# Who subtracts the low parts of the weights: GpSimd or VectorE, in a two-layer hybrid decoder step

## The chip, the cores and the metric

The kernel is one program on one core of a Trainium2 chip. The metric is the device time of one execution in microseconds (us); three runs of the kernel before gave 2476.75, 2478.96 and 2480.17, and their median, 2478.96, is the time before.

## What is computed

Two layers, each of them: a half-step SwiGLU feed-forward, a token mixing step, another half-step SwiGLU. The mixing step multiplies the normed input by one wide matrix and cuts the product into parts: z, the 4096 convolution channels (x, B, C), dt, the attention's q, k, v and two gates. The convolution channels feed a state-space scan (SSD); q, k, v feed a dilated window attention; both results are gated, added and multiplied by a last matrix.

```python
z, xbc, dt_raw, q, k, v, g_ssd, g_attn = split_cols(u @ w_in, IN_SIZES)
conv = silu(conv_b + sum(xbc_full[:, i:i + seqlen] * conv_w[i] for i in range(4)))
y, new_ssm = ssd_scan(xs5, dt, a_head, bmat, cmat, ssm_state)     # 8 groups of 4 heads
y = grouped_rmsnorm((y + d_skip * xs5) * silu(z), ssd_norm, 8)
merged = sigmoid(g_ssd) * (y @ w_ssd_out) + sigmoid(g_attn) * (attn @ w_attn_out)
return merged @ w_o, ...
```

All is float32. There are 256 prompt tokens and 32 tokens of the second group, 288 columns in all.

## The kernel before

The weights pass through the core once. They come in *units* of 128 x 2048 numbers (1 MB), two at a time in the two slots s = 0 and 1 of `raw`, `w_hi` and `w_lo`. A unit's way is always the same, and each step has a semaphore of its own per slot:

- SP loads it into `raw[s]` once the low part of the slot's last unit is made (`unit`, L494 to L498, waits for `lo_ready[s]`).
- ScalarE rounds it into `w_hi[s]` once TensorE is done with the slot's last unit (`high_unit`, L669 to L672; signal `hi_ready[s]`).
- An engine subtracts, `w_lo = raw - w_hi` (`low_unit`; signal `lo_ready[s]`). VectorE has one at L920 to L924, GpSimd has another at L1334 to L1337.
- TensorE multiplies (`product`, L1412 to L1417): three matmuls for each block, `w_hi` by the input's high part, `w_hi` by its low part, `w_lo` by its high part. At the end it signals `unit_done[s]`.

While TensorE works on one slot, the other slot's next unit is prepared. Every engine runs its own list in order; nothing is reordered, and a wait holds all that stands behind it on the engine. The order is written out by hand.

A layer passes through these stages: the first feed-forward; q, k, v and dt; the convolution channels (16 units, `xbc`, between steps of the attention); eight state-space groups (each with three half units of z and gate columns, `side`); a tail (gate units, the sums for the grouped norm, the attention's output matrix, four pairs of `w_ssd_out`, two of `w_o`); the second feed-forward.

In the feed-forwards and the q, k, v stage VectorE makes all low parts. In the other stages GpSimd makes many:

- Convolution: VectorE's `xbc(n)` (L1088) makes the unit of slot 0 at its head when n is even; GpSimd loops over the eight units of slot 1 (L1377). `xbc(n)` then copies the convolution's tails (L1092) and applies four taps to two channel tiles (L1103 the first, L1106 the rest); its last tap lets ScalarE apply silu (L738). At the stage's end ScalarE's copies to `conv_out` (L827) stand behind the last silu.
- Groups: all units by GpSimd (`side_low`, L1386), one after each group and one more in odd groups, between its output DMAs (L1396 of the prompt's state, L1400 of the sample states).
- Tail: all units by GpSimd, in a loop of nine pairs (L1402).

VectorE's part of one group (from L1200) is, in order: `a_tri` (L1207 to L1214) for TensorE's product L1779; `xdt`, `cbm`, `xdte` (L1222 to L1235); for the group before, rows times silu of z (`times_z`, L1194 to L1198); `b_diag` (L1242); the decay matrices times `cbm` (L1248, L1250, signal `m_ready`), for which TensorE's product L1799 waits; then the outputs (L1255 to L1264), the new states (L1271) and the sample rows (L1276 to L1282), which let the next group start. ScalarE makes the exponentials for L1248 from the result of L1779 to L1784; meanwhile TensorE has the matmul L1790 and a half unit.

In the tail VectorE makes `y` ready in four parts: reciprocal (L1294), four scalings (L1297), split into high and low (L933, L935). After the second part it waits for the attention's output product and multiplies it with its gate (L1305). After the last pair of `w_ssd_out` come the merging (L1312, L1317, split), the residual sum (`add_to_x`, L985), the next norm (L954, L958, L950).

Of the kernel before, what the change touches and what calls it, by code (L numbers as in the profile page):

```python
# [40 lines left out]
G = 8  # L41
# [33 lines left out]
PAIRS_SO, PAIRS_AO, PAIRS_WO = 4, 1, 2  # L75
# [3 lines left out]
M_XBC = M_QKV + PAIRS_QKV  # L79
# [104 lines left out]
def trunk(nc, x_prompt, x_sample, cache_kv_w128, cache_kv_w512, cache_kv_w2048, state_conv, state_ssm,  # L184
# [163 lines left out]
    with ExitStack() as ctx:  # L348
# [570 lines left out]
        def _(dve):  # L919
# [87 lines left out]
            with dve.Fori(0, DEPTH) as l:  # L1007
# [78 lines left out]


                def xbc(n):  # L1088
                    if n % 2 == 0:
                        low_unit(0, m + (M_XBC + n // 2 + 1))  # L1090
                    wait(dve, xbc_taken, l, 2 * n + 2)
                    dve.tensor_copy(tails[:, 2 * n:2 * n + 2], flat[:, 2 * n:2 * n + 2, TP:TP + 9 * RUN]  # L1092
                                    .rearrange("p t (j c) -> p t j c", c=RUN)[:, :, :, 0:CW - 1])\
                        .then_inc(tails_ready.sem, 1)
                    if n:
                        wait(dve, xbc_ready, l, n)
                    for w in range(CW):
                        for t in range(2):
                            tile = 2 * n + t
                            src, dst = flat[:, tile, w:w + CONVED], acc[:, t, 0:CONVED]  # L1100
                            tap = conv_wt[:, w * KC + tile:w * KC + tile + 1]
                            if w == 0:
                                dve.tensor_scalar(dst, src, tap, vecs[:, V_CONVB + tile:V_CONVB + tile + 1],  # L1103
                                                  ALU.mult, ALU.add)
                            else:
                                last = dve.scalar_tensor_tensor(out=dst, in0=src, scalar=tap, in1=dst,  # L1106
                                                                op0=ALU.mult, op1=ALU.add)
                        if w < CW - 1:
                            dve.drain()
                    last.then_inc(conv_ready.sem, 1)  # L1110
# [83 lines left out]
                def times_z(g):  # L1194

                    wait(dve, silu_z_ready, l, g + 1)
                    rows_y = flat[:, 2 * g:2 * g + 2, 0:T]
                    dve.tensor_tensor(rows_y, rows_y, silu_z[:], ALU.mult).then_inc(z_used.sem, 1)  # L1198

                for g in range(G):  # L1200
                    heads = slice(HPG * g, HPG * g + HPG)

# [35 lines left out]
                        .then_inc(xdt_ready.sem, 1)  # L1238
                    if g:
                        times_z(g - 1)  # L1240
                    wait(dve, b_ready, l, g + 1)
                    dve.tensor_tensor(b_diag[:], b_tm_s[:].unsqueeze(1).broadcast_to((TS, NB, NS)),  # L1242
                                      sel_s.unsqueeze(2).broadcast_to((TS, NB, NS)), ALU.mult)\
# [3 lines left out]
                    for c in range(2):  # L1247
# [2 lines left out]
                    dve.tensor_tensor(dec_s[:], dec_s[:], cbm_s[:].unsqueeze(1).broadcast_to((TS, HPG, TS)), ALU.mult)\  # L1250
                        .then_inc(m_ready.sem, 1)

                    wait(dve, y_product, l, g + 1)
                    off = ps[:, 1, 0:256].rearrange("p (t c) -> p t c", t=2)
                    dve.tensor_tensor(off_t[:], off, e_off[:], ALU.mult)  # L1255
# [29 lines left out]
                    last.then_inc(y_read.sem, 1)  # L1285
                dve.drain().then_inc(rows_used.sem, 1)
                times_z(G - 1)

                wait(dve, y_rms_ready, l, 1)
                wait(dve, conv_done_out, l, 32)  # L1290
                wait(dve, h_end_out, l, 16 * G)
                for n in range(PAIRS_SO):
# [8 lines left out]
                    if n == 1:  # L1301

                        wait(dve, unit_done[1], l, M_AO + 1)
                        for o in range(0, KD, 2):
                            dve.tensor_tensor(gates[:, KD + o:KD + o + 2, :], ps[:, o:o + 2, 0:T],  # L1305
                                              gates[:, KD + o:KD + o + 2, :], ALU.mult).then_inc(row_evac.sem, 1)


                wait(dve, gates_ready, l, 1)
                wait(dve, unit_done[1], l, M_SO + PAIRS_SO)  # L1310
# [4 lines left out]
                for n in range(2 * PAIRS_WO):  # L1315
                    tiles = slice(2 * n, 2 * n + 2)
                    dve.tensor_tensor(merged[:, tiles], merged[:, tiles], gates[:, KD + 2 * n:KD + 2 * n + 2, :],  # L1317
                                      ALU.add)
                    split(mg_hi[:, tiles], mg_lo[:, tiles], merged[:, tiles]).then_inc(merged_ready.sem, 1)
                add_to_x(l, M_WO + PAIRS_WO, 1.0)  # L1320
                norm(l, 3, V_F2)
                swiglu(l, M_W13B, E_W13B, PAIRS_W13)

            dve.wait_ge(end_rms.sem, 1)
# [7 lines left out]
        @block.gpsimd  # L1332
        def _(pool):
            def low_unit(s, m):  # L1334
                pool.wait_ge(hi_ready[s].sem, m + 1)
                pool.tensor_tensor(w_lo[s][:], raw[s][:], w_hi[s][:].bitcast(F32), ALU.subtract)\  # L1336
                    .then_inc(lo_ready[s].sem, 1)  # L1337


            for s in range(2):  # L1340
                pool.sem_inc(lo_ready[s].sem, 1)
                pool.sem_inc(unit_done[s].sem, 1)
                pool.sem_inc(evac[s].sem, 1)
            pool.sem_inc(vec_turned.sem, 1)
            pool.sem_inc(rows_used.sem, 1)
            pool.sem_inc(row_evac.sem, 4)

            pool.wait_ge(start_in.sem, 16 * 9)
            for g in range(NG):
                last = pool.tensor_tensor(rel_q[:, g], delta[:], rel4[:, 4 * g:4 * g + 4].unsqueeze(1).unsqueeze(3)  # L1350
                                          .broadcast_to((P, NB, HPG, NT)), ALU.mult)
            last.then_inc(rel_q_ready.sem, 1)
            low_unit(0, 0)

            pool.wait_ge(lines_ready.sem, 1)
            pool.dma_start(lines_dram.rearrange("(g i) w -> i g w", g=NG), lines[:]).then_inc(lines_out.sem, 16)
            pool.wait_ge(lines_out.sem, 16)
            pool.dma_start(skewed.rearrange("h (p w) -> h p w", p=P)[:, :, 0:W_LINE],
                           bass.AP(lines_dram.tensor, lines_dram.offset,
                                   [[W_LINE, NG * HPG], [0, P], [1, W_LINE]])).then_inc(skewed_out.sem, 16)  # L1360
            pool.wait_ge(skewed_out.sem, 16)
            for h in range(NG * HPG):

                src = skewed[h, 0:P * W_LINE].rearrange("(p w) -> p w", p=P)[:, P - 1:P - 1 + 2 * P]
                pool.dma_start(bias_p[:, h, :], src).then_inc(bias_in.sem, 16)
            with pool.Fori(0, DEPTH) as l:
                m = l * PAIRS

                wait(pool, kv_copied, l, 9)
                for g in range(NG):  # L1370
                    c0 = 1 if g == 0 else 0
                    dst = kv_prompt[g][bass.ds(l, 1), 0].rearrange("a (c p) k h e -> p (a c) (k h e)", p=P)
                    pool.dma_start(dst, kv_p[:, c0:, g].rearrange("p c k e -> p c (k e)"))\  # L1373
                        .then_inc(kv_out.sem, 16)
                    dst = kv_sample[g][bass.ds(l, 1)].rearrange("a b t k h e -> (a b t) (k h e)")
                    pool.dma_start(dst, kv_s[:, g].rearrange("p k e -> p (k e)")).then_inc(kv_out.sem, 16)
                with pool.Fori(0, PAIRS_XBC) as i:  # L1377
                    low_unit(1, m + (M_XBC + 1 + i))

                wait(pool, tails_copied, l, 8)  # L1380
                pool.dma_start(conv_prompt[bass.ds(l, 1), 0].rearrange("a i c -> (a i) c"), conv_out[0:3, :])\
                    .then_inc(conv_done_out.sem, 16)
                pool.dma_start(conv_sample[bass.ds(l, 1)].rearrange("a b i c -> (a b i) c"), conv_out[3:27, :])\
                    .then_inc(conv_done_out.sem, 16)

                def side_low(n):  # L1386
                    low_unit(n % 2, m + (M_SIDE + n // 2))

                for g in range(G):
                    if g % 2:  # L1390
                        side_low(3 * g // 2 + 2)
                    wait(pool, h_end_ready, l, g + 1)
                    dst = ssm_prompt[bass.ds(l, 1), 0, HPG * g:HPG * g + HPG]\
                        .rearrange("a h p n -> (a h p) n")\
                        .rearrange("(t q) n -> q t n", t=2)
                    pool.dma_start(dst, h_end[:]).then_inc(h_end_out.sem, 16)  # L1396
                    for t in (2 * g, 2 * g + 1):
                        wait(pool, h_new_ready, l, t + 1)
                        dst = ssm_sample[bass.ds(l, 1), :, 2 * t:2 * t + 2].rearrange("a b h p n -> (a h p) b n")
                        pool.dma_start(dst, h0[t % 3][:]).then_inc(h_new_out[t % 3].sem, 16)  # L1400
                    side_low((3 * g + 1) // 2 + 2)
                with pool.Fori(PAIRS_SIDE, PAIRS_SIDE + PAIRS_G + PAIRS_SO + PAIRS_AO + PAIRS_WO) as i:  # L1402
                    for s in range(2):
                        low_unit(s, m + (M_SIDE + 1 + i))

            for signal in (kv_out, conv_done_out, h_end_out, *h_new_out):
                pool.wait_ge(signal.sem, DEPTH * signal.per)
# [513 lines left out]
```

## Time and profile before

| | |
|---|---|
| profiled execution, span | 2479.5 us |
| median of three runs | 2478.96 us |
| TensorE (PE) busy | 2237.7 us, 90% |
| VectorE (DVE) busy | 1291.6 us, 52% |
| ScalarE (ACT) busy | 985.0 us, 40% |
| GpSimd (POOL) busy | 417.0 us, 17% |
| mean granted clock of TensorE | 0.920 |

The profiled execution's own time is its span. Busy time is the time in which an instruction of the engine runs; time in which such an instruction is held up inside the engine counts as busy too. [...] In a row of a timeline the brackets hold the engine's idle time before the instruction and what ended it.

### The profile page before, as it was taken

To read this page: it belongs to the slowest core of one execution; us is meant where nothing else is said; L and a number is where in the kernel's file an instruction comes from. 1 tells how busy PE (TensorE), PEld (TensorE's weight loads), DVE (VectorE), ACT (ScalarE), POOL (GpSimd) and SP (SyncE) were. 2 spreads that over 40 slices of the span, in tenths; PEclk is the share of its full clock that TensorE was granted. 3 is DMA by queue.
4 is the path that set the end of the run, shared out by engine and by line. 5 is a ranking of instruction groups with operands and counts; after the bars stand their busy time and mean duration, and the time that the engine had idled before them with its cause. 6 is when DMAs were issued, how large, how long until landed. Compare 5 with 4: busy or idle time off the path is not lost.

```text
span 2479.5 us, 38482 instructions
## 1 busy us (share of the span) xinstructions
PE 2237.7 (90%) x15036; PEld 2079.1 (84%) x15036; DVE 1291.6 (52%) x1936; ACT 985.0 (40%) x1121; POOL 417.0 (17%) x162
## 2 busy tenths in 40 slices
PE   7999899988898888899989989999798889869996
PEld 5999889976677788799889989898677778869996
DVE  3553546665656472454355453576665663544543
ACT  3552434253333432454255434343432334325532
POOL 2000002211222355200000000121122223640000
PEclk9999989789888889999999999897988889989998
DMA  7444543413433333344444437442233332434441
GB/s 200 160 165 139 177 149 123 132 52 103 123 92 105 96 103 126 124 158 152 155 129 159 160 120 206 137 132 84 84 99 98 105 115 71 150 107 141 162 157 65
DMA packets 258231, 317.05 MB, mean 128 GB/s; under 512 B 9070, under 2 KB 232846, under 8 KB 258010
## 3 DMA queue, kind: packets, MB, share of 16 engines
q1 hardware_dynamic: 249656, 287.92, 36.4%
q0 software_dynamic: 7776, 26.73, 3.6%
q8 instruction: 76, 1.25, 0.2%
q10 hardware_dynamic: 680, 0.80, 0.1%
q14 instruction: 43, 0.35, 0.0%
HBM read 291.44 MB, written 26.33 MB: 128 GB/s over the span
## 4 chain that ended last, share of the span: by engine, by line
PE 72%; DVE 11%; PEld 5%; ACT 4%; issue 3%; POOL 3%; DVEq 1%; DMA 1%; SPq 0%; PEldq 0%; ACTq 0%; POOLq 0%
PE ps L1415 18%; PE ps L1417 17%; PE ps L1416 17%; PE ps L1516 4%; POOL w_lo L1336 3%; PE ps L1836 2%; PE ps L1832 2%; ACT w_hi L672 2%; DVE a_tri L1207 2%; DVE w_lo L923 1%; PE ps L1779 1%; PEld ps L1415 1%; PEld ps L1691 1%; PE ps L1500 1%; PEld ps L1417 1%
## 5 line engine op out<-in xcount | busy, mean ns | idle before, releaser
L1415 PE MATMUL ps<-u_hi,w_hi 128*128 128x288 f32 x2736 | 866.5, 317 | 50.0 <-DVE u_lo L950 39.7
L1416 PE MATMUL ps<-u_lo,w_hi 128*128 128x288 f32 x2736 | 848.3, 310 | 0.0
L1417 PE MATMUL ps<-u_hi,w_lo 128*128 128x288 f32 x2736 | 845.1, 309 | 0.0
L672 ACT ACTIVATE w_hi<-w_raw 128x2048 fp32r<-128x2048 f32 x249 | 476.2, 1912 | 660.7 <-PE ps L1417 634.8
L923 DVE TENSOR_TENSOR w_lo<-w_raw,w_hi 128x2048 fp32r<-128x2048 f32 x172 | 394.3, 2292 | 547.2 <-ACT w_hi L672 547.1
L1415 PEld LDWEIGHTS ps<-u_hi,w_hi 128*128 128x128 f32 x2736 | 554.7, 203 | 57.3 <-issue 53.7
L1416 PEld LDWEIGHTS ps<-u_lo,w_hi 128*128 128x128 f32 x2736 | 555.8, 203 | 0.5
L1417 PEld LDWEIGHTS ps<-u_hi,w_lo 128*128 128x128 f32 x2736 | 554.8, 203 | 0.0
L1336 POOL TENSOR_TENSOR w_lo<-w_raw,w_hi 128x2048 fp32r<-128x2048 f32 x77 | 358.0, 4649 | 626.0 <-ACT w_hi L672 625.8
L1415 PE MATMUL ps<-h_hi,w_hi 128*128 (+1 forms) x704 | 209.2, 297 | 14.6 <-DVE w_lo L923 14.6
L1417 PE MATMUL ps<-h_hi,w_lo 128*128 (+1 forms) x704 | 207.9, 295 | 0.0
L1416 PE MATMUL ps<-h_lo,w_hi 128*128 (+1 forms) x704 | 207.8, 295 | 0.0
L1415 PEld LDWEIGHTS ps<-h_hi,w_hi 128*128 128x128 f32 x704 | 132.8, 189 | 17.4 <-DVE w_lo L923 11.5
L1373 POOL DMA_DIRECT2D out_dram<-kv_p x6 | 4.1, 680 | 850.0 <-DVE kv_s L1085 849.8
L1416 PEld LDWEIGHTS ps<-h_lo,w_hi 128*128 128x128 f32 x704 | 132.9, 189 | 0.0
L1417 PEld LDWEIGHTS ps<-h_hi,w_lo 128*128 128x128 f32 x704 | 132.7, 188 | 0.0
L1271 DVE SCALAR_TENSOR_TENSOR h<-h,e_s,ps 128x128 f32<-128x128 f32 x256 | 69.0, 341 | 113.1 <-PE ps L1836 112.4
L1106 DVE SCALAR_TENSOR_TENSOR acc<-flat,conv_wt,acc 128x312 f32<-128x312 f32 x192 | 104.4, 585 | 7.3
L1415 PE MATMUL ps<-y_hi,w_hi 128*128 128x288 f32 (+1 forms) x256 | 79.3, 310 | 9.7 <-POOL w_lo L1336 9.7
L672 ACT ACT_TABLE_LOAD x45 | 57.7, 1283 | 71.1 <-DMA w_raw<-in_ffn_w_dram 71.1
L1836 PEld LDWEIGHTS ps<-flat,h_t 128*128 128x128 f32 x512 | 60.7, 195 | 24.3 <-ACT h_t L872 12.1
L1416 PE MATMUL ps<-y_lo,w_hi 128*128 128x288 f32 (+1 forms) x256 | 77.9, 304 | 0.0
(270 smaller groups left out, 2803.6 us busy)
## 6 DMA issues: line engine op xcount, KB each, us to landing
w_raw<-in_ffn_w_dram SPq DMA_DIRECT2D x128, 1024.0 KB, 5.0
w_raw<-in_w_in_dram SPq DMA_DIRECT2D x82, 1024.0 KB, 5.3
h<-in_state_ssm_dram SPq DMA_DIRECT2D x32, 512.0 KB, 4.1
out_dram<-h POOLq DMA_DIRECT2D x32, 512.0 KB, 3.8
w_raw<-in_w_ssd_out_dram SPq DMA_DIRECT2D x16, 1024.0 KB, 4.9
kv_in<-in_cache_kv_w_dram SPq DMA_DIRECT2D x32, 256.0 KB, 4.1
w_raw<-in_w_o_dram SPq DMA_DIRECT2D x8, 1024.0 KB, 5.0
w_raw<-in_ffn_w_dram SPq DMA_DIRECT2D x8, 512.0 KB, 3.5
```

What stands on the lines that cost most here:

```text
L672: act.activation(w_hi[s][:], raw[s][:], ACT.Copy).then_inc(hi_ready[s].sem, 1)
L923: dve.tensor_tensor(w_lo[s][:], raw[s][:], w_hi[s][:].bitcast(F32), ALU.subtract)\
L1106: last = dve.scalar_tensor_tensor(out=dst, in0=src, scalar=tap, in1=dst, op0=ALU.mult, op1=ALU.add)
L1207: dve.tensor_scalar(a_tri[c][:, h, :], tri, da[:, c, HPG * g + h:HPG * g + h + 1], None, ALU.mult)
L1271: dve.scalar_tensor_tensor(out=h0[tile % 3][:, b, :], in0=h0[tile % 3][:, b, :], scalar=e_s[:, t, TS + b:TS + b + 1], in1=ps[:, 6 + b // 4 ...
L1336: pool.tensor_tensor(w_lo[s][:], raw[s][:], w_hi[s][:].bitcast(F32), ALU.subtract)\
L1415: pe.matmul(out, wh, hi, start=first, stop=False)
L1416: pe.matmul(out, wh, lo, start=False, stop=False)
L1417: return pe.matmul(out, wl, hi, start=False, stop=last)
L1516: return pe.transpose(out, src, square[0:p, 0, 0:p])
L1832: pe.matmul(ps[:, 6 + n, :], xdte_s[:, t * P:(t + 1) * P], b_diag[:, 4 * n:4 * n + 4, :].rearrange("p b n -> p (b n)"), start=True, stop=True)
L1836: last = pe.matmul(ps[:, 3 - 2 * t, 320 + b * NT:320 + (b + 1) * NT], h0_t[:, b, :], fc[:, TP + b * NT:TP + (b + 1) * NT], start=True, sto ...
```

## The change

The subtraction of 76 of the 77 units that GpSimd makes goes to VectorE; GpSimd keeps the very first unit of the program and its output DMAs. The places on VectorE are:

- convolution: in every `xbc(n)` after the second of the four taps, for both slots; the low unit at the head of even n goes;
- groups: from group 1 on, one after `times_z`, ahead of `b_diag`; in odd groups one more between `m_ready` and the wait for `y_product`; one after the last group, followed by the pair M_G + 1;
- tail: a pair after each of the four parts of `y` (after the second part behind the gate products), a pair and one unit ahead of the merging, single units between the four merging steps, one ahead of the residual sum and one behind the next norm.

```diff
                 def xbc(n):
-                    if n % 2 == 0:
-                        low_unit(0, m + (M_XBC + n // 2 + 1))
                     wait(dve, xbc_taken, l, 2 * n + 2)
...
                                 last = dve.scalar_tensor_tensor(out=dst, in0=src, scalar=tap, in1=dst,
                                                                 op0=ALU.mult, op1=ALU.add)
+                        if w == 1:
+                            low_unit(n % 2, m + (M_XBC + n // 2 + 1))
                         if w < CW - 1:
                             dve.drain()
...
+                def side_low(n):
+                    low_unit(n % 2, m + (M_SIDE + n // 2))
...
                     if g:
                         times_z(g - 1)
+                        side_low((3 * g - 2) // 2 + 2)
                     wait(dve, b_ready, l, g + 1)
...
+                    if g % 2:
+                        side_low(3 * g // 2 + 2)
                     wait(dve, y_product, l, g + 1)
...
                 times_z(G - 1)
+                side_low((3 * G - 2) // 2 + 2)
+                low(m + (M_G + 1))
...
-
+                    low(m + (M_AO + n))
+                low(m + (M_SO + PAIRS_SO - 1))
+                low_unit(0, m + M_WO)
...
+                    if n == 0:
+                        low_unit(1, m + M_WO)
+                    elif n >= 2:
+                        low_unit(n % 2, m + (M_WO + 1))
+                low_unit(0, m + M_W13B)
                 add_to_x(l, M_WO + PAIRS_WO, 1.0)
                 norm(l, 3, V_F2)
+                low_unit(1, m + M_W13B)
...
-                with pool.Fori(0, PAIRS_XBC) as i:
-                    low_unit(1, m + (M_XBC + 1 + i))
...
-                    if g % 2:
-                        side_low(3 * g // 2 + 2)
...
-                    side_low((3 * g + 1) // 2 + 2)
-                with pool.Fori(PAIRS_SIDE, PAIRS_SIDE + PAIRS_G + PAIRS_SO + PAIRS_AO + PAIRS_WO) as i:
-                    for s in range(2):
-                        low_unit(s, m + (M_SIDE + 1 + i))
```

## Rows read from the trace of the kernel before

**Rows 1.** Stretches: length; busy (x) of PE, PEld, DVE, ACT, POOL; clock, DMA, GB/s.

```profile
569.29:853.69 284.40, 255.91 (x1561) 207.11 (x1561) 170.98 (x441) 93.00 (x154) 72.60 (x37) 0.87 0.34 103
1784.51:2068.91 284.40, 255.76 (x1562) 207.71 (x1563) 170.97 (x441) 93.16 (x154) 73.56 (x37) 0.88 0.34 103
569.29:600.21 30.92, 30.92 (x195) 25.30 (x196) 14.71 (x43) 10.77 (x18) 4.52 (x6) 0.90 0.30 83
596.20:599.60 3.40, 3.40 (x16) 3.40 (x16) 3.13 (x11) 0.00 (x0) 1.15 (x2) 0.50 0.49 145
862.50:865.90 3.40, 3.40 (x28) 3.40 (x27) 0.00 (x0) 2.59 (x3) 2.67 (x1) 1.00 0.84 251
```

**Rows 2.** Waits, whole run: who waited for whom, us in total, times, longest.

```profile
ACT flat L738 <- DVE acc L1106: 28.1, 6, 8.6
PE ps L1779 <- DVE a_exp_s L1214: 27.2, 7, 4.4
PE ps L1415 <- DVE merged_lo L935: 17.6, 2, 8.8
PE ps L1799 <- DVE dec_s L1250: 15.9, 5, 3.2
PE ps L1415 <- POOL w_lo L1336: 13.6, 14, 3.4
PE ps L1516 <- DVE flat L1282: 8.9, 2, 5.1
PE ps L1790 <- DVE xdte_s L1235: 3.5, 1, 3.5
```

**Rows 3.** Single lines of the kernel: count, least, median and greatest duration in ns.

```profile
L1336 POOL TENSOR_TENSOR w_lo<-w_raw,w_hi x77: 4495/4587/5476, 18.9 to 2225.1; 128x2048 fp32r<-128x2048 f32 x77
L923 DVE TENSOR_TENSOR w_lo<-w_raw,w_hi x172: 2271/2293/2296, 41.1 to 2447.6; 128x2048 fp32r<-128x2048 f32 x172
L1207 DVE TENSOR_SCALAR a_tri<-square,da x128: 267/275/5398, 564.2 to 2035.3; 128x128 f32<-128x128 f32 x128
L1242 DVE TENSOR_TENSOR b_diag<-b_tm_s,small x16: 1205/1206/5604, 575.5 to 2040.1; 32x1024 f32<-32x1024 f32 x16
L1317 DVE TENSOR_TENSOR merged<-merged,flat x8: 749/752/4315, 967.1 to 2191.8; 128x576 f32<-128x576 f32 x8
L958 DVE SCALAR_TENSOR_TENSOR full<-x,vecs,rinv x48: 504/509/4611, 34.8 to 2233.8; 128x288 f32<-128x288 f32 x48
```

**Rows 4.** Timeline of VectorE in group 2: start us, us, instruction.

```profile
642.18 0.74 DVE L1198 TENSOR_TENSOR flat<-flat,silu_z 128x576 f32<-128x576 f32 x1
642.85 5.60 DVE L1242 TENSOR_TENSOR b_diag<-b_tm_s,small 32x1024 f32<-32x1024 f32 x1
648.39 1.28 DVE L1248 TENSOR_TENSOR dec<-dec,cbm 128x512 f32<-128x512 f32 x2
```

**Rows 5.** Timeline of GpSimd in the same group.

```profile
641.92 5.46 POOL L1336 TENSOR_TENSOR w_lo<-w_raw,w_hi 128x2048 fp32r<-128x2048 f32 x1 [5.41 <-ACT w_hi L672]
```

**Rows 6.** Timeline of TensorE in the same group, and at the tail's first `w_ssd_out` unit.

```profile
639.09 1.98 PE L1779 MATMUL ps<-a_tri,square 128*128 128x512 f32 x4
...
649.92 1.14 PE L1799 MATMUL ps<-dec,xdt 128*64 128x128 f32 x16 [3.19 <-DVE dec_s L1250]
...
907.86 0.61 PE L1415 MATMUL ps<-y_hi,w_hi 128*128 128x288 f32 x1 [3.43 <-POOL w_lo L1336]
```

**Rows 7.** Timeline of ScalarE: a high part in group 2, another in the tail.

```profile
639.95 1.89 ACT L672 ACTIVATE w_hi<-w_raw 128x2048 fp32r<-128x2048 f32 x1
...
893.58 1.91 ACT L672 ACTIVATE w_hi<-w_raw 128x2048 fp32r<-128x2048 f32 x1 [2.58 <-PE ps L1417]
```

**Rows 8.** Timeline of VectorE in the tail: a part of `y`, the gate products.

```profile
878.70 3.75 DVE L1294 RECIPROCAL y_rms<-y_rms 128x576 f32<-128x576 f32 x1 [22.57 <-ACT y_rms L897]
...
885.24 1.36 DVE L935 TENSOR_TENSOR y_lo<-flat,y_hi 128x1152 fp32r<-128x1152 f32 x1
...
904.47 2.75 DVE L1305 TENSOR_TENSOR flat<-ps,flat 128x576 f32<-128x576 f32 x4 [2.65 <-PE ps L1417]
```

More of the change, by code:

```diff
@@ L1366, in _ @@
             with pool.Fori(0, DEPTH) as l:
-                m = l * PAIRS
                 wait(pool, kv_copied, l, 9)
@@ L1384, in _ @@
                     .then_inc(conv_done_out.sem, 16)
-                def side_low(n):
-                    low_unit(n % 2, m + (M_SIDE + n // 2))
                 for g in range(G):
-                    if g % 2:
-                        side_low(3 * g // 2 + 2)
                     wait(pool, h_end_ready, l, g + 1)
```

## The prediction, made before the changed kernel was run

> **What bounds the kernel now.** I read the page's busy times first, then the stretches, the waits of TensorE, the single lines, and last the timelines of one state-space group and of the tail.
>
> The busy times show TensorE busy nearly all the time, so a gain can only come from its idle gaps and from stretches at the half clock. Group 0 of layer 0 lasts 30.92 us and TensorE is busy in all of it; all eight groups take 284.40, in both layers [rows 1]. So the other seven average (284.40 - 30.92) / 7 = 36.21 us for the same work.
>
> The waits tell what the seven lack: TensorE waited on VectorE's `a_tri` group (27.2 us), on `dec_s` (15.9), on `flat` (8.9) and on `xdte_s` (3.5), together 55.5 us in fifteen waits [rows 2]. VectorE is not short of time there: it is busy in 171 of 284 us [rows 1].
>
> Why it is late shows in single lines. L1242 takes 1206 ns in the median and 5604 at most, L1207 275 and 5398, L1317 752 and 4315, L958 509 and 4611 [rows 3]. In group 2 the long L1242 starts at 642.85, inside GpSimd's subtraction of 641.92 to 647.38, and ends at 648.45, 1.07 us behind it, about its own 1.21 [rows 4, 5]. So I read the long rows as an instruction of VectorE that is held until GpSimd's subtraction ends. TensorE's L1799 then starts 3.19 us late [rows 6].
>
> The tail has gaps of its own: 13.6 us behind GpSimd's low parts and 17.6 behind the merging, over two layers [rows 2].
>
> **The change part by part.** A subtraction takes 2293 ns on VectorE against 4587 on GpSimd [rows 3]. VectorE gets 76 of them, 174 us of work, and loses the holds. Both layers look alike, so I cost one layer and double it.
>
> *Groups.* Removed: the holds, which stretch seven groups by 36.21 - 30.92 = 5.29 us each, half-clock time after the gaps included. Added: a low unit between L1198 and L1242. In group 2, count from L1779's start at 639.09 [rows 6]. L1198 ends at 642.92, 3.83 us after that [rows 4]. The unit's high part was ready at 641.84, at 2.75 [rows 7], so the low unit runs to 6.12; L1242 with its 1.21 ends at 7.33; the decay products took 649.92 - 648.39 = 1.53 up to TensorE's start [rows 4, 6], so L1799 may start at 8.86. TensorE is ready for it at 649.92 - 3.19 = 646.73, at 7.64 [rows 6]. A new wait of 1.2, with semaphores 1.3 us. Queued behind the low unit are `b_diag` (needed later) and the decay products, for which TensorE waits. The second low unit of odd groups stands ahead of the wait for `y_product`; it delays the outputs, whose next consumer comes after two more products, so I cost it at nothing; if that cover is gone it costs up to 2.29 in four groups. Sum: 7 x (5.29 - 1.3) = 28.0 us per layer gained. The trace of before does not show this wait; its bounds are 0 (the low unit fits in the time in which VectorE waits for ScalarE's exponentials) and a full 2.29 plus a spell at half clock, 3.40 x 0.50 = 1.7 [rows 1], so 7 x 1.3 = 9 to 7 x 5.29 = 37. I take 1.3, since every term but the order has its row; I put the likely ends at 20 and 34.
>
> *Convolution.* Even units only move within `xbc`. Odd ones came from GpSimd and also held VectorE, so 2.29 us of work replaces a hold, mostly off TensorE's path. The last, in `xbc(15)`, is on it: ScalarE's silu waits there for VectorE's last tap (8.6 us, the longest such wait [rows 2]), ScalarE's conv_out copies stand behind it, and TensorE waits for those. Cost 2.3 per layer, bounds 0 and 4.6 (two units on the path).
>
> *Tail.* Gone: GpSimd's waits, 13.6 / 2 = 6.8 per layer, of which 3.43 stand before the first `w_ssd_out` unit at 907.86 [rows 2, 6]. The hold in the merging, 4315 - 752 = 3.56, and the one in the next norm, 4611 - 509 = 4.10 [rows 3]; both have TensorE waiting behind them. Added: VectorE's order. The second of the pair after part one of `y` waits for ScalarE's high part, ready at 895.49 [rows 7], some 1.8 earlier after the first gap is gone (an estimate: the 6.8 less 3.43 and a series of small ones leave about 1.6 to 1.8 for it), so at 893.7. Then: that low unit to 896.0; the second part of `y`, as long as the first, 878.70 to 886.60 = 7.90 [rows 8], to 903.9; the gate products, 2.75 [rows 8], to 906.65; one more low unit to 908.95. So the first `w_ssd_out` unit starts 1.1 later than its 907.86 although everything ahead of it came earlier. A further 1.5 I allow for one pair of `w_ssd_out` whose low unit stands behind a part of `y` (bounds 0 and 2.29). Balance: + 1.1 + 1.5, less the small GpSimd waits behind 907.86 (about 1.75), less 3.56, less 4.10: 6.8 us gained per layer; bounds 2.3 (the norm and merging gain less two waits of 2.7) and 10.4.
>
> *Nothing.* GpSimd's DMAs lose the subtractions ahead of them in its queue and issue earlier; slots are free for SP's loads 2.3 earlier in the tail and at about the same time in the groups; the load was no wait of TensorE. Both at zero.
>
> Sum per layer: 28.0 - 2.3 + 6.8 = 32.5, twice 65. The profiled execution has 2479.5 and the median is 2479.0, so 2479 - 65 = **2414**. The likely case's own ends: 20 - 4.6 + 2.3 = 17.7 and 34 + 10.4 = 44.4 per layer, so 2444 and 2390.
>
> [...]
>
> **The rivals.**
> *The clock stays full once the gaps are gone.* Then group 0's loss, 0.10 x 30.92 = 3.1 us, would vanish from eight groups of both layers, 50 us more: 2364. Against it: the 0.50 row without a gap. [...]
> *Each new wait halves the clock.* As after the old gaps: 14 waits of 1.3 each lose 1.7 more, 24 us: 2438. For it: the eight groups ran at 0.87 in the mean, group 0, which had no gap, at 0.90. Against: 14 waits for GpSimd's low parts, 1.0 us in the mean, lie in the two tails [rows 2], and the stretch at 862.5, behind the first of them, ran at 1.00 [rows 1].
> *VectorE's order turns slower.* The low unit ahead of `b_diag` waits for ScalarE's high part, and everything behind it waits too. In group 2 the part is there 1.08 us ahead of VectorE. Each us beyond costs 14 us in all (seven groups, two layers), so from 65 / 14 = 4.7 beyond the margin the kernel is slower; with 7 it is 2414 + 98 = 2512. For it: in even groups the part comes only 2.75 after L1779's start, behind a silu. Against: nothing in the change delays that part.
> *The holds do not come from GpSimd.* Then the long rows stay and only new waits come: 2 x (7 x 1.3 + 2.3 + 2.6) = 28, 2507. Against: VectorE's own subtraction, which in this kernel lies in stages without GpSimd's, is 2271 to 2296 in all 172 rows [rows 3].
>
> **How the numbers follow.** Forecast 2414 with 0.62; half clock after each wait 0.20; full clock 0.05; slower by order 0.07; holds of another origin 0.03; gain eaten to about nothing by several new waits 0.03. About 0.2% (5 us) is what a measurement here tells from no change. Faster 0.87, same 0.03, slower 0.10. The range takes in the first two cases and the bounds, 2388 to 2448; outside it are the other cases, 0.18.
>
> **What would show it right or wrong.** Right: the maxima of L1207, L1242, L1317 and L958 fall to their medians; the waits on `a_exp_s`, `flat` and `xdte_s` go or fall under 1 us each; L1799 waits 1.0 to 1.6 us on `dec_s` in groups 1 to 7; groups last 31.5 to 33; TensorE's wait for ScalarE's conv_out grows by about 2.3 in each layer; the norm's first unit follows the residual sum 4 us sooner. Wrong: long rows of VectorE without GpSimd beside them; waits of L923 for ScalarE's high part in the groups; a wait over 2.3 us at L1799; a tail as long as before.

## The result, and the profile after

The changed kernel takes 2408.76 us (median of four, 2402.76 to 2417.88) against 2478.11 before on the same chip: a ratio of 0.9715, with a 95% interval of 0.9693 to 0.9737, so 69 us less. The forecast was 2414, with 2388 to 2448. The profiled execution of after has a span of 2407.2; the one of before had 2479.5.

The page first: busy times.

```profile
PE 2212.2 (92%) x15036; PEld 2063.8 (86%) x15036; DVE 1279.2 (53%) x2012; ACT 984.7 (41%) x1121; POOL 63.7 (3%) x86
```

VectorE does 76 subtractions more than before, some 174 us of work, and yet its busy time is shorter: 1279.2 us against 1291.6, and in the groups of one layer 152.40 against 170.98 [rows 1], with eleven low parts more in that stretch. An instruction that is held counts as busy, as `b_diag` does in [rows 4] with 5.60 us for its 1.21; a good part of the busy time of before was holding.

The stretches of the eight groups (length; busy of PE, PEld, DVE, ACT, POOL; clock, DMA, GB/s), then three single groups of layer 0 (0, 1 and 5). The clock is the granted clock, TensorE's share of its full speed in the stretch:

```profile
571.59:827.26 255.67, 247.29 (x1560) 202.88 (x1560) 152.40 (x452) 92.78 (x154) 21.18 (x26) 0.90 0.38 114
1751.82:2008.67 256.85, 247.76 (x1560) 203.95 (x1560) 152.36 (x452) 92.82 (x154) 21.19 (x26) 0.90 0.38 114
...
571.59:605.30 33.71, 33.71 (x195) 27.43 (x196) 14.35 (x49) 10.76 (x18) 3.61 (x5) 0.82 0.28 78
605.30:635.85 30.55, 29.56 (x198) 24.18 (x197) 21.07 (x61) 9.21 (x17) 2.51 (x3) 0.94 0.37 108
729.15:762.04 32.89, 31.26 (x197) 25.81 (x196) 22.28 (x67) 9.20 (x17) 3.31 (x4) 0.90 0.33 100
```

TensorE's idle time in the groups of layer 0 falls from 284.40 - 255.91 = 28.5 to 255.67 - 247.29 = 8.4 us, and its busy time for the same work by 8.6, at a mean clock of 0.90 instead of 0.87. In layer 1 the second stretch of [rows 1] is cut a little behind its instructions: from their starts, 1784.44 and 2068.64, it lasts 284.20 and not 284.40.

Five lines of TensorE's waits, whole run (total, times, longest), and the single lines that answer to [rows 3]:

```profile
PE ps L1417 <- DVE w_lo L923: 35.3, 20, 6.4
PE ps L1801 <- DVE dec_s L1254: 13.2, 14, 1.0
PE ps L1518 <- ACT conv_out L827: 11.4, 2, 5.9
PE ps L1417 <- DVE merged_lo L935: 10.6, 2, 5.3
PE ps L1781 <- DVE a_exp_s L1217: 2.7, 3, 0.9
```

```profile
L1210 DVE TENSOR_SCALAR a_tri<-square,da x128: 268/279/596, 566.5 to 1976.2; 128x128 f32<-128x128 f32 x128
L1246 DVE TENSOR_TENSOR b_diag<-b_tm_s,small x16: 1205/1206/1207, 577.9 to 1983.2; 32x1024 f32<-32x1024 f32 x16
L1327 DVE TENSOR_TENSOR merged<-merged,flat x8: 750/752/758, 940.8 to 2135.0; 128x576 f32<-128x576 f32 x8
L958 DVE SCALAR_TENSOR_TENSOR full<-x,vecs,rinv x48: 510/514/520, 35.3 to 2162.6; 128x288 f32<-128x288 f32 x48
L923 DVE TENSOR_TENSOR w_lo<-w_raw,w_hi x248: 2272/2292/2296, 41.6 to 2375.3; 128x2048 fp32r<-128x2048 f32 x124
```

Against [rows 2, 3]: the long rows are gone (596 instead of 5398, 1207 instead of 5604, 758 instead of 4315, 520 instead of 4611). The waits on `flat`, on `xdte_s` and on GpSimd's low parts are gone, the one on `a_exp_s` is a tenth of what it was. What stands in their place is 14 waits on `dec_s`, one in each group but the first, and waits for VectorE's low parts in the tails: 16.0 us in four waits there, where GpSimd's had 13.6 in fourteen [rows 2].

From the starts of the same instructions in both traces, the two layers are shorter by 28.7 and 27.3 us in the groups and by 8.0 and 11.2 from there to the first unit behind the last norm, and longer by 1.3 and 2.3 from the turn of dt to the first group. That is 71.6 of the 72.3 us between the two spans.

### The profile page after: what moved, and what is told of

It reads as the page before. It is cut to its first block, busy times and chain, and to the rows that moved or that the text cites. A ratio compares the mean times of both kernels' runs of the same rounds, so it can differ in the third digit from the quotient of the medians.

```text
span 2407.2 us, 38390 instructions
## 1 busy us (share of the span) xinstructions
PE 2212.2 (92%) x15036; PEld 2063.8 (86%) x15036; DVE 1279.2 (53%) x2012; ACT 984.7 (41%) x1121; POOL 63.7 (3%) x86
## 4 chain that ended last, share of the span: by engine, by line
PE 73%; DVE 12%; PEld 5%; ACT 4%; issue 2%; DVEq 2%; DMA 1%; SPq 0%; PEldq 0%; ACTq 0%
PE ps L1417 19%; PE ps L1419 18%; PE ps L1418 18%; DVE w_lo L923 4%; PE ps L1518 4%; PE ps L1838 3%; PE ps L1834 3%; ACT w_hi L672 2%; PE ps L1502 1%; PEld ps L1417 1%; PEld ps L1693 1%; PEld ps L1419 1%; PEld ps L1418 1%; PE ps L1639 1%; PE ps L1495 1%
## 5 line engine op out<-in xcount | busy, mean ns | idle before, releaser
L923 DVE TENSOR_TENSOR w_lo<-w_raw,w_hi 128x2048 fp32r<-128x2048 f32 x248 | 567.8, 2290 | 608.3 <-ACT w_hi L672 608.3
L1104 DVE SCALAR_TENSOR_TENSOR acc<-flat,conv_wt,acc 128x312 f32<-128x312 f32 x192 | 95.8, 541 | 8.6 <-issue 0.9
L750 ACT ACTIVATE flat<-ps 128x32 f32<-128x32 f32 x64 | 12.7, 199 | 167.9 <-PE ps L1419 167.8
L1419 PE MATMUL ps<-y_hi,w_lo 128*128 128x288 f32 (+1 forms) x256 | 77.2, 302 | 0.0
```

Source lines behind the costliest of these rows:

```text
L923: dve.tensor_tensor(w_lo[s][:], raw[s][:], w_hi[s][:].bitcast(F32), ALU.subtract)\
L1419: return pe.matmul(out, wl, hi, start=False, stop=last)
```

## The experiments

Theory, *hold*: VectorE's instructions are held while GpSimd subtracts; the gain is the end of that. Rivals: *speed*, a low part is ready 2.3 us sooner; *queue*, GpSimd's output transfers no longer stand behind subtractions.

### GpSimd subtracts as before, for nobody (e_dummy)

The edit in short, against the changed kernel (`constant` stands for a view of the constant tile `square`):

```diff
+ pad = nc.alloc_sbuf_tensor_at("pad", [P, KC, 2 * PITCH], bfloat16, offset=F_AT)[:, :, 2 * T:]   # unused columns of flat
+ def dummy_unit(s, m):                       # on GpSimd, where low_unit stood in groups and tail
+     pool.wait_ge(hi_ready[s].sem, m + 1)
+     pool.tensor_tensor(pad, constant, constant, ALU.subtract).then_inc(dummy_done.sem, 1)
```

> The changed kernel, in which GpSimd subtracts all the same: at the 12 places of the groups and at 16 of the 18 of the tail of each layer it waits for the same high part as before and then subtracts 128 x 2048 numbers of a constant from themselves, into columns that nothing reads, and nobody waits for the result during that work. The low parts are VectorE's, as in the changed kernel. Theory 'hold' (VectorE's operations are held while GpSimd subtracts): the long rows of before come back (a_tri and b_diag with maxima near 5.4 and 5.6 us) although every low part is still VectorE's; the groups give back their 57 us of two layers or more, since VectorE's own subtraction is now held too, and the tail most of its 20: 2465 to 2510 us. Rival 'speed' (the gain is that a low part is ready 2.3 us sooner): nothing returns, 2404 to 2414. Rival 'queue' (the gain is that GpSimd's output transfers no longer stand behind subtractions): 2440 to 2480, but the maxima of a_tri and b_diag stay under 2 us.

Measured: 2513.59 us, ratio 1.012 (1.0095 to 1.0146): the whole gain is gone and 33 us more. The lines (count, least, median, greatest ns), then the timeline of one group (start, us, instruction, idle time before it and its releaser):

```profile
L1364 POOL TENSOR_TENSOR pad<-square x56: 3593/5700/6669, 610.9 to 2247.1; 128x2048 bf16<-128x2048 f32 x56
L1248 DVE TENSOR_TENSOR b_diag<-b_tm_s,small x16: 1204/1206/4610, 579.9 to 2068.0; 32x1024 f32<-32x1024 f32 x16
L1237 DVE TENSOR_TENSOR xdte<-xdt,to_end x48: 410/418/3834, 578.6 to 2064.5; 128x256 f32<-128x256 f32 x48
L925 DVE TENSOR_TENSOR w_lo<-w_raw,w_hi x248: 2271/2292/5689, 41.3 to 2486.5; 128x2048 fp32r<-128x2048 f32 x124
```

```profile
646.58 6.67 POOL L1364 TENSOR_TENSOR pad<-square 128x2048 bf16<-128x2048 f32 x1 [5.42 <-ACT w_hi L674]
646.84 0.74 DVE L1200 TENSOR_TENSOR flat<-flat,silu_z 128x576 f32<-128x576 f32 x1
647.51 2.27 DVE L925 TENSOR_TENSOR w_lo<-w_raw,w_hi 128x2048 fp32r<-128x2048 f32 x1
649.72 4.61 DVE L1248 TENSOR_TENSOR b_diag<-b_tm_s,small 32x1024 f32<-32x1024 f32 x1
...
655.78 0.48 PE L1824 MATMUL ps<-dec,xdt 128*64 128x128 f32 x2 [4.40 <-DVE dec_s L1256]
```

*Speed* is out: every low part was VectorE's and the time came back. `b_diag` of 1.21 us takes 4.61 and ends at 654.33, 1.08 behind GpSimd's end at 653.25, and TensorE waits 4.40 us: the chain of [rows 4 to 6] once more, without any data going from GpSimd to VectorE. My expectation missed twice: `a_tri` is not among the held lines here (GpSimd was done before the next group), and the time lies 4 us above its range, although it had counted VectorE's own low parts as held too, which they are (5689 against 2296 at most).

The row above also shows the other direction: the subtraction of 3.59 us (the least) took 6.67. It began 0.26 us before L1200, while VectorE's operations ran back to back and took no longer than elsewhere, and lost 3.08 us: 646.58 + 3.08 = 649.66, about the end of L925 at 649.78. So I read GpSimd's subtraction as held first, and `b_diag` after that.

### GpSimd writes instead of subtracting (e_fill)

Against e_dummy, in short:

```diff
-     pool.tensor_tensor(pad, constant, constant, ALU.subtract)
+     pool.tensor_tensor(pad[:, 0, 0:1], ident[:, 0:1], ident[:, 0:1], ALU.subtract)   # one element; carries the wait
+     pool.memset(pad, 0.0)
```

> As the kernel with GpSimd's dead subtractions, but GpSimd writes zeros into the same unused columns instead: it reads no two operands, waits for the same high part (in a subtraction of one element), and is as much in its own queue's way, or a little less. If VectorE is held by whatever GpSimd does in its memory: the maxima of b_diag and xdte return and the time goes to 2450 or more. If only an operation of GpSimd with two operands in that memory holds it: maxima as in the changed kernel, 2403 to 2418; that would also show that the waiting in GpSimd's queue costs nothing.

Measured: 2410.55 us, ratio 0.9718 (0.9703 to 0.9733), the changed kernel's.

```profile
L1364 POOL MEMSET pad<- x56: 1798/1804/2405, 608.3 to 2144.0; 128x2048 bf16 x56
L1362 POOL TENSOR_TENSOR pad<-square x56: 190/2299/3267, 608.0 to 2141.6; 128x1 bf16<-128x1 f32 x56
L1248 DVE TENSOR_TENSOR b_diag<-b_tm_s,small x16: 1205/1206/1207, 577.4 to 1980.5; 32x1024 f32<-32x1024 f32 x16
```

A fill of the same extent leaves VectorE's instructions with two operands alone: `b_diag` keeps its 1207 ns, `xdte` and the low parts, beside which fills ran too, stay at 426 and 2296 at most. And the subtraction of one element, 190 ns at least, takes 2299 in the median: about the time of VectorE's low part (2292), which starts on the same high part. So for these instructions it is GpSimd's operation with operands to read that holds them and is held by them in these runs, not GpSimd being busy.

A fill does hold instructions of another kind. VectorE's casts, which read one operand, waited for it (the line of one, then a fill and a cast in the tail):

```profile
L935 DVE CAST merged_hi<-merged x8: 460/596/1550, 937.4 to 2138.2; 128x576 fp32r<-128x576 f32 x8
...
952.91 1.80 POOL L1364 MEMSET pad<- 128x2048 bf16 x1
953.48 1.55 DVE L935 CAST merged_hi<-merged 128x576 fp32r<-128x576 f32 x1
```

In the changed kernel this cast takes 461 ns at most. The two fills of 2.36 and 2.41 us started beside a cast. These holds are few, and the time does not show them.

*Queue* gets no support: the output transfers stood behind 56 waits for high parts and some 3.5 us of work each, and the time did not move. (The fill, 1.80 us, is shorter than the dead subtraction, 3.59 at least, so a delay of its full length was not tried.) What no run here shows is why a fill and a cast wait for each other (up to 1550 ns for 460) while `b_diag` runs beside fills in its 1207, and why `a_tri`, with one tensor to read, was held in before (5398 ns for 275).

### The three parts alone (e_groups, e_tail, e_conv)

Each is the kernel before with one of the diff's three parts: its low parts taken from GpSimd's program and put into VectorE's where the change puts them.

> The kernel before with only the low parts of the groups (12 per layer) moved to VectorE, as the change places them; convolution and tail stay with GpSimd. 'Hold': the 14 held groups lose 4.1 us each, net of the new wait for dec_s, so 56 to 58 us: 2418 to 2425. 'Speed' alone would give at most what TensorE waits for low parts in the groups of before, under 10 us: 2468 to 2478. If the parts of the change help or hurt each other (clock, queue), the three partial kernels don't sum to the 69 us of the whole.

> The kernel before with only the tail's low parts (18 per layer) moved to VectorE; convolution and groups stay with GpSimd. From the stages of the two traces: -1.6 (first weights behind the groups), -3.6 (merging), -4.1 (norm), +2.7 (first unit of w_ssd_out), -1 to -3 for the rest: 8 to 11 us per layer, 16 to 22 in all: 2456 to 2462. If instead VectorE's order in the tail costs what GpSimd's did: 2474 to 2482.

> The kernel before with only the convolution's 8 low parts per layer moved to VectorE. Its last low part stands ahead of the last taps, +2.2 us per layer at the end of the convolution, and -0.5 per layer ahead of it: 2480 to 2484, a small loss. If the holds of the convolution bound it, a gain of 2 us or more: below 2476.

| part alone | us | ratio (95%) | against before (2480.78) | forecast, both layers |
|---|---|---|---|---|
| groups | 2415.39 | 0.9735 (0.9717 to 0.9753) | -65.4 | -56.0 |
| tail | 2463.23 | 0.9925 (0.9909 to 0.9940) | -17.6 | -13.6 |
| convolution | 2485.71 | 1.0019 (1.0010 to 1.0028) | +4.9 | +4.6 |

The signs and the order of the sizes are the forecast's, and the convolution's part is a loss, as costed. What I expected of the single runs was a little off in all three: the groups came out 2.6 us under their range, the tail 1.2 and the convolution 1.7 above theirs. The parts sum to 78 us less; the whole gives 69 to 73 in two comparisons. The intervals are 2 to 6 us wide to either side, so the gap of 5 to 9 is not shown to be more than scatter.

### What the new waits cost (after_again, e_mready, e_order, e_last)

Three edits of the changed kernel, each at a place where the prediction had put a cost, and the changed kernel itself as base. The code is shortened, and e_order is told as the order of its calls.

```diff
  # e_mready: the first low part of a group behind dec_s
                     if g:
                         times_z(g - 1)
-                        side_low((3 * g - 2) // 2 + 2)
...
                         .then_inc(m_ready.sem, 1)
+                    if g:
+                        side_low((3 * g - 2) // 2 + 2)
  # e_last, in xbc(n): the last low part behind the last taps
-                        if w == 1:
+                        if w == 1 and n < XBC_UNITS - 1:
                             low_unit(n % 2, m + (M_XBC + n // 2 + 1))
...
                     last.then_inc(conv_ready.sem, 1)
+                    if n == XBC_UNITS - 1:
+                        low_unit(n % 2, m + (M_XBC + n // 2 + 1))
  # e_order: VectorE's order in the tail (root = the reciprocal, scaled = scalings and split)
- root(0) scaled(0) low(M_AO) | root(1) scaled(1) gates low(M_SO) | root(2) scaled(2) low(M_SO+1) | root(3) scaled(3)
+ root(0) scaled(0) low_unit(0, M_AO) root(1) low_unit(1, M_AO) scaled(1) low_unit(0, M_SO) gates low_unit(1, M_SO)
+ root(2) scaled(2) low_unit(0, M_SO+1) root(3) low_unit(1, M_SO+1) scaled(3)
```

> The changed kernel once more, beside the next three on the same chip, as their base: 2403 to 2418 us.

> The changed kernel with the first low part of each group after the first moved from ahead of b_diag, dec and dec_s to behind dec_s, so that it runs while TensorE multiplies dec and dec_s. Theory: the 14 waits of TensorE on dec_s (13.2 us in the trace of the changed kernel) are VectorE's 2.3 us low part ahead of dec_s and go; the low part is ready 1.6 us later and nobody waits for it: 13 us less than the changed kernel beside it, 2390 to 2402. Rival: the later low part lets its weights arrive later and TensorE waits for w_lo or w_hi in the groups instead, or off_t comes late in the groups that have two low parts: 0 to 6 us less. Rival 'clock': the shorter group changes how long TensorE is granted the half clock, by up to 15 us either way.

> The changed kernel with the tail's VectorE operations in another order: the root's reciprocal of the second and of the fourth part of y stand between two low parts (in idle time), and the first low part of w_ssd_out stands ahead of the four gate products. Theory: TensorE's 6.4 us wait ahead of the first unit of w_ssd_out shortens by 2.6 and the 1.8 us wait ahead of its fifth unit goes: 4.4 us per layer, 8 to 9 us less than the changed kernel beside it. Rival: the first unit waits for the gate products (the banks they free), which now end later by the low part that stands ahead of them: 2 to 5 us less only.

> The changed kernel with only the convolution's last low part moved behind its last taps. Theory: the path last taps, silu, groups gets the 2.2 us per layer back that the change had cost: 4.5 us less than the changed kernel (2408), 2400 to 2407. The kernel with all three edits came out 16 us below what the other two sum to; if that is this edit's doing, for instance because TensorE enters the groups at another clock: 2390 to 2395.

| kernel | us | ratio to before (95%) | less than after_again |
|---|---|---|---|
| after_again | 2408.26 | 0.9717 (0.9695 to 0.9740) | |
| e_mready | 2395.84 | 0.9655 (0.9637 to 0.9674) | 12.4 |
| e_order | 2400.09 | 0.9672 (0.9658 to 0.9685) | 8.2 |
| e_last | 2404.77 | 0.9691 (0.9677 to 0.9706) | 3.5 |

The three costs came out near the sizes expected of these runs. For e_mready and e_order the intervals are clear of after_again's; e_last's is not, and there the trace decides: the stretch that the low part had lengthened, from TensorE's turn of the tails to the first group, is back from 10.89 to 8.68 and 8.67 us. But look at e_mready's rows: two lines of TensorE's waits, the eight groups of both layers, and one group of layer 0 at a clock of 0.94.

```profile
PE ps L1418 <- DVE w_lo L923: 34.8, 21, 6.3
PE ps L1782 <- DVE a_exp_s L1217: 7.2, 8, 0.9
...
571.03:824.68 253.65, 249.11 (x1560) 204.54 (x1561) 152.76 (x452) 92.85 (x154) 21.25 (x26) 0.89 0.38 115
1749.04:1999.14 250.10, 245.70 (x1560) 201.46 (x1561) 152.76 (x452) 92.85 (x154) 21.23 (x26) 0.91 0.38 115
...
670.34:700.86 30.52, 29.63 (x198) 24.25 (x196) 22.38 (x67) 9.21 (x17) 3.14 (x4) 0.94 0.37 112
```

The wait on `dec_s` is gone from all 14 groups, yet a group at a clock of 0.94 lasts 30.52 instead of 30.55: in it the wait has moved to `a_exp_s`, at the group's head (0.89). TensorE's idle time in the groups falls from 17.5 to 8.9 us, 8.6 rather than 13.2. The next thing late is VectorE's own chain from a group's last state to the next group's `a_tri`, and only groups with more time at the half clock, where TensorE is slower than that chain, got shorter (at 0.89 from 32.22 to 31.27). In the trace of e_mready its 128x288 matmuls start 0.24 us apart at a clock of 0.50 (from 720.67) and 0.13 at 1.00 (from 739.57). I had read 13.2 us of waits as 13.2 us of time; the 12.4 measured has another 4 us in it, within the scatter of the medians, that these rows don't name.

In e_order the wait ahead of the first `w_ssd_out` unit, after and then e_order:

```profile
882.08 0.61 PE L1417 MATMUL ps<-y_hi,w_hi 128*128 128x288 f32 x1 [6.37 <-DVE w_lo L923]
```

```profile
882.62 0.60 PE L1432 MATMUL ps<-y_hi,w_hi 128*128 128x288 f32 x1 [3.88 <-DVE flat L1321]
```

It is 2.5 us shorter and has changed its releaser: the gate products, behind the low part that now stands ahead of them. The rival named that wait; its price was the theory's, as the wait of 1.77 ahead of the fifth unit is gone too.

### Together, and in pairs (e_all, e_mready_last, e_mready_order)

> Both of these edits, and the convolution's last low part moved behind its last tap (2.2 us per layer): if the three lie in different stages they add, 13 + 8.5 + 4.5 = 26 us less than the changed kernel beside it, 2377 to 2390. If the clock gives back part of it, 2390 to 2400.

> The changed kernel with the groups' first low part behind dec_s and the convolution's last low part behind its last taps, without the tail's order. Alone these two gave 12.4 and 3.5 us, all three together 37.1 where the three singles sum to 24.1. If this pair interacts (the groups are entered 2.2 us earlier, without the spell at the lower clock in the first group): 29 us less than the changed kernel, 2377 to 2382. If it only adds: 16 less, 2390 to 2395.

> The changed kernel with the groups' first low part behind dec_s and the tail's order, without the convolution's edit. Alone 12.4 and 8.2. If groups and tail interact: 33 us less than the changed kernel, 2373 to 2378; if they only add: 20.6 less, 2386 to 2391.

| kernel | us | ratio to before (95%) | less than after_again | sum of the singles |
|---|---|---|---|---|
| e_all | 2371.13 | 0.9554 (0.9532 to 0.9576) | 37.1 | 24.1 |
| e_mready_last | 2385.46 | 0.9611 (0.9595 to 0.9626) | 22.8 | 15.9 |
| e_mready_order | 2380.52 | 0.9604 (0.9588 to 0.9621) | 27.7 | 20.6 |

e_all beats both kernels: 37 us under the changed one, 110 under the one before, and 6 under the range that I gave it. Its groups, and its first two of layer 0:

```profile
569.97:819.27 249.30, 244.78 (x1560) 201.31 (x1561) 152.75 (x452) 92.81 (x154) 21.19 (x26) 0.91 0.41 123
1733.95:1983.28 249.33, 244.80 (x1560) 201.33 (x1560) 152.76 (x452) 92.81 (x154) 21.20 (x26) 0.91 0.41 123
...
569.97:599.49 29.52, 29.52 (x196) 24.21 (x197) 14.38 (x49) 10.77 (x18) 3.61 (x5) 0.94 0.46 137
599.49:633.68 34.19, 34.19 (x197) 28.89 (x196) 21.63 (x64) 9.21 (x17) 2.51 (x3) 0.80 0.34 101
```

Neither pair showed the 29 or the 33 that an interaction of that pair alone would give; by the medians each lies 7 us above its sum and the three together 13. That the edits give more than their sum is not shown. The base enters each sum of singles more than once, and its interval alone is some 5 us wide to either side. By the ratios, which set each kernel against the one before in its own comparison, the excess is smaller: the singles give 0.9655 + 0.9672 + 0.9691 - 2 x 0.9717 = 0.9584 and e_all has 0.9554, 7 us less; for the pairs the excess is 4.5 and 1.5 us. And the two profiled executions, 2404.13 of after_again and 2378.51 of e_all, lie 25.6 us apart, near the sum of 24.1. The clock moves such numbers: against e_mready, e_all's groups have the same idle time (498.6 - 489.6 = 9.0 us in both layers against 8.9) and 5.2 us less busy time for the same work, and two profiles of the changed kernel differ by 4 to 6 us in the groups of a single layer.

## Why the prediction was right

*The mechanism* is shown, not only inferred: the long rows of two-operand instructions are gone with the subtractions, back with dead ones (e_dummy), absent with fills (e_fill). In before, 46 instructions of VectorE took over two and a half times their line's median, and each ran beside one of GpSimd's subtractions. The 0.03 for holds of another origin is out. The ground given against it was not quite right: the convolution has subtractions of both engines. But none of VectorE's 172 ran beside one of GpSimd's in before, so their even 2271 to 2296 ns say nothing either way.

*Groups*: 28.0 per layer, measured 28.7 and 27.3. The count from L1779's start held nearly term by term. Group 2 of after, TensorE and VectorE (start, us, instruction):

```profile
637.54 1.98 PE L1781 MATMUL ps<-a_tri,square 128*128 128x512 f32 x4
...
640.64 0.74 DVE L1198 TENSOR_TENSOR flat<-flat,silu_z 128x576 f32<-128x576 f32 x1
641.31 2.27 DVE L923 TENSOR_TENSOR w_lo<-w_raw,w_hi 128x2048 fp32r<-128x2048 f32 x1
643.51 1.21 DVE L1246 TENSOR_TENSOR b_diag<-b_tm_s,small 32x1024 f32<-32x1024 f32 x1
644.65 1.27 DVE L1252 TENSOR_TENSOR dec<-dec,cbm 128x512 f32<-128x512 f32 x2
...
646.18 1.09 PE L1801 MATMUL ps<-dec,xdt 128*64 128x128 f32 x16 [1.00 <-DVE dec_s L1254]
```

Counted from L1781's start: TensorE ready for L1801 at 7.64 by the forecast, 7.64 measured (646.18 less the wait of 1.00); the products' start at 8.86, measured 8.64. So the wait is 0.74 to 1.00 in the 14 groups and not 1.3: each of L923, L1246 and L1252 starts 0.07 before the row ahead of it ends, which makes the 0.22, and the rest is my allowance for semaphores, which no row gives. The margin of ScalarE's high part held as well: L923 waits for none in that group. The low unit ahead of `y_product`, costed at nothing, cost nothing that the waits show: none of TensorE's is on `off_t`, and the three on `a_exp_s` stand at the head of groups 5 and 7, behind groups that have no such unit.

That the sum of the groups came out within 1 us in each layer is partly luck. The forecast left group 0 as it was and gave each of the seven others 30.92 + 1.3 = 32.2 us. In layer 0, group 0 grew from 30.92 to 33.71 at a clock of 0.82 instead of 0.90, for which the sum had nothing, and the others average 31.7. With the same wait of 1.0 us a group lasts 30.5, 32.2 or 33.6, at 0.94, 0.89 and 0.85 (groups 2, 4 and 3, the last of layer 1), not at one clock, as the sum had it with group 0's 30.92 at 0.90 for all of them. The same kernel once more, after_again, has 259.91 and 251.26 us in the groups, 24.5 and 32.9 less than before. Over both layers the two profiles agree better, 56.1 and 57.4 for the 56.0 forecast.

*What failed inside the right sum* is that I took each wait of the 14 as so much time. e_mready shows that at a clock of 0.94 the same group without that wait is as long, since `a_exp_s` is late next. A stall's price is the distance to what is late next, and that row has to be looked for even when the sum comes out.

*Convolution*: 2.3 per layer; TensorE's stretch from the turn of the tails to the first group grew from 8.67 to 10.89 in both layers, 2.22. e_conv gave +4.9 for both layers, and e_last took the 2.2 back in each. The sign that I had given for it failed: the wait for `conv_out` itself grew only from 10.0 to 11.4 in both layers, as the turn of the tails ahead of it took 5.00 and 5.38 instead of 3.65 us.

*Tail*: 6.8 per layer, measured 8.0 and 11.2; the second lies above the bound of 10.4. Its large terms hold: merging 3.55 (3.56 forecast; the wait on `merged_lo` falls from 17.6 in [rows 2] to 10.6), norm 4.09 (4.10). The pair behind a part of `y` has a wait of 1.77 against 1.5. Mis-sized are the smaller terms. The first `w_ssd_out` unit, counted from the end of the groups, came 0.64 later in one layer and 0.68 sooner in the other, against 1.1 later forecast. The stretch from that unit to the merging lost 0.56 and 1.74 (0.25 forecast), and `w_o` with what follows lost 0.46 and 1.14, for which the sum had nothing. Nearly all of the difference between the layers at the first unit is the clock's: the stretch of the second pair of gate units, the same work in both, takes 17.13 us at 0.90 in one layer and 15.83 at 1.00 in the other. For the rest no row of after tells the change from the clock.

*The clock*. "Each new wait halves the clock" is out: groups 1 and 5 have a wait at L1801 each and show 0.94 and 0.90, group 0 has none and shows 0.82. "The clock stays full" is out too: groups 0 of after and 1 of e_all ran at 0.82 and 0.80 with TensorE busy in all of them. Row 596.20:599.60 [rows 1] says the same: 0.50 with TensorE busy in all of its 3.40 us, in a group without an idle gap. These three rows have a lowered clock and no gap, and the 2364 that stood on a full clock lies 45 us under the result. What lowers the clock no run here shows.

*Slower by VectorE's order*: the low unit ahead of `b_diag` waited for ScalarE's high part in no group. The second one of the odd groups did, in all eight of them, for 1.3 to 1.6 us; group 1 of layer 0:

```profile
616.92 2.29 DVE L923 TENSOR_TENSOR w_lo<-w_raw,w_hi 128x2048 fp32r<-128x2048 f32 x1 [1.34 <-ACT w_hi L672]
```

I had named such waits as a sign of being wrong, without telling the two units apart. They stand behind `dec_s`, and no wait of TensorE follows from them. In the tail another order is worth 8.2 us (e_order): there VectorE's order was a cost, which the sum had counted in at the first `w_ssd_out` unit and the pair, and it did not make the kernel slower.

## What to carry to other kernels

When an instruction of one engine now and then takes several times its median, lay the other engines' timelines beside it before calling it slow: here its end followed another engine's end by about its own length (1.07 and 1.08 us for 1.21), and moving the other engine's work over made the first engine less busy. Place moved work behind the operation that signals the critical consumer, and into idle time between two waits, not ahead of it: three such moves were worth another 37 us. And price a wait by what is late next, which only a run without the wait shows.

## What the runs showed of the hardware that I had not expected

- The hold goes both ways. GpSimd's subtraction of 3.59 us took up to 6.67 beside VectorE's, and one of a single element, 0.19 us, took 2.30 in the median.
- GpSimd's fill of 128 x 2048 (1.80 us) ran beside VectorE's two-operand work and left it as it was: `b_diag` stayed at 1205 to 1207 ns. Beside VectorE's casts one waited for the other: a cast of 0.46 us took up to 1.55, a fill up to 2.41.
- TensorE ran groups of 34 us at a mean clock of 0.80 to 0.82 without one idle gap (1 of e_all, 34.19 us; 0 of after, 33.71), and groups with a gap of 1.0 us at 0.94 (1 and 2 of after, 30.55 and 30.54).
